# Seven-product B section in the last block, and weight-sum stores issued by GpSimd

## The chip, the cores and the metric

The kernel runs on one core of one Trainium2 chip. The metric is the device time of one execution in microseconds (us). The engines are TensorE (PE), VectorE (DVE), ScalarE (ACT), GpSimd (POOL) and SyncE (SP, which only issues DMAs here). Each engine works through its own instructions in order. They meet through semaphores.

## The reference, cut to what matters

One layer of a streaming encoder over 2048 prompt tokens and 64 sample tokens:

```
h = rmsnorm(x); proj = h @ w_in                       # 1024 -> 10240 columns
a_u,a_v,a_z, b_a,b_b,b_z, c_x,c_z, d_b,d_c,d_x,d_z, gate_logits = split(proj)
glu = b_a * sigmoid(b_b)                              # the "B" section
cb = causal_depthwise(glu, 31 taps); out_b = silu(layernorm(cb)) * silu(b_z)
...                                                   # three more branches
merged = sum_i sigmoid(gates_i) * (out_i @ w_branch_i); y = merged @ w_out
x = x + rmsnorm(y)
```

## The kernel before, in words

The tokens go in four blocks of 512 (the last one 576, with the 64 sample tokens), j = 0 to 3 in the code, called blocks one to four here. A block is 120 *units* on PE. A unit is one product of a 1024x128 weight tile with the block's activations, in three passes (high part by high part, high by low, low by high), 24 matmuls of 512 columns. A *half unit* has a 512x128 weight and 12 matmuls. The units form sections in this order: B (8 units), V (4), C (8), M (8), G0 (16, full and half alternating), D (16), G1 (16), G2 (12), Z (4), G2b (4), G3 (16), O (8). The B section gives b_a and b_b, whose product with the sigmoid is `glu`. DVE then runs the 31 taps of the depthwise convolution (`conv_step`, four DVE instructions a tap, eight in block four) wherever it has room.

From M to G3, blocks three and four use a seven-product scheme (Strassen's, in Winograd's form) in place of plain units: a *pair* of units becomes seven products of 12 matmuls with half the tokens as columns, 84 matmuls where the units need 96 of the same width. DVE adds the products in `pair_sums` (seven adds, five of which read PSUM), ACT copies the first product out of PSUM (`copy_p1`). The scheme needs sums of the activations (`t_sums`, high and low parts made by ACT and DVE in section O of the block before) and sums of the weights.

The weight sums are made once, in 60 *halves* (30 pairs by two). For each half SP loads the raw weights (`s_load`, 512 KB), POOL forms four sums (`s_sums`, four instructions), ACT casts them to the high part (`s_cast`), POOL subtracts for the low part (`s_low`), and SP stores both (`s_store`, 1 MB) to `s_parts` in DRAM, from where blocks three and four load them as `chunk`s of 512 KB through a ring of eight. Eight halves are made in block one (`HALF0`), 52 in block two, one about every two units. The order is written out by hand: lists such as `HALF_LOAD`, `HALF_STORE`, `HALF_CAST` hold, for each half, the step (a unit number) at which an engine does its part. SP's queue in block two is, step by step: the due store, the due raw load, the unit's weight load (`split_load`, up to four units ahead). A half's sums wait until the last store from the same `s_out` buffer has landed.

Of the kernel before, what the change touches and what calls it, by code (L numbers as in the profile page):

```python
# [19 lines left out]
P = 128  # L20
# [37 lines left out]
NPAIR = len(PAIRS)  # L58
NCHUNK = PAIR_CHUNK[-1]
# [7 lines left out]
NH = 2 * NPAIR  # L67
HW = WB // 2
# [6 lines left out]
SUM0 = [UNIT0["G0"] + r for r in (1, 7, 13)] + [UNIT0["G3"] - 1 + 5 * h for h in range(5)]  # L75
# [19 lines left out]
RAW_OF = [0 if h < HALF0 else (h - HALF0) % 3 for h in range(NH)]  # L95
SUM_OF = [0 if h < HALF0 else (h - HALF0) % 2 for h in range(NH)]

# [41 lines left out]

def unit_pieces(name, r):  # L140

    if name[0] == "G":
        m = GATED[name][1] + r // 2
        if r % 2:
            return [("branch", GATED[name][0] * KT + m, 0)]
        return [("main", MAIN0[name] + r // 2, c) for c in range(2)]
    return [("main", MAIN0[name] + r, c) for c in range(2)]


def chunk_stream():  # L150
# [7 lines left out]
    for j in range(SEVEN0, NBLK):  # L158
        if j > SEVEN0:
            for name, count in SECTIONS:  # L160
                if name == "M":
                    break
                for r in range(count):
# [28 lines left out]
def build(nc, x_t, x_rows, w_main, w_half, w_branch, cols, rows, bs_rows, ws_t, mask_t, pool_w, ident_in,  # L192
# [4 lines left out]
    def sb(name, shape, dt=F32, addr=None):  # L197
# [3 lines left out]
        if addr is None:  # L201
# [23 lines left out]
    s_parts = nc.dram_tensor("s_parts", (NPAIR, 2, P, 4, 2, HW), F32).ap()  # L225
# [34 lines left out]
    s_out = [sb(f"s_out{b}", [P, 4, 2, HW], F32R, addr=o) for b, o in enumerate((t2_at, raw_at))]  # L260
    s_sum = [sb(f"s_sum{b}", [P, 4, 2, HW], addr=o) for b, o in enumerate((t2_at, raw_at))]
# [3 lines left out]
             enumerate([o + TPB // 2 * DM * 4 for o in out1_at] + [at[0], at[0] + HW * 4])]  # L265
    zc = [sb(f"zc{b}", [P, WMAX]) for b in range(2)]

    a = at[0]
    ext = [sb(f"ext{b}", [P, EL]) for b in range(2)]
    sq_x = sb("sq_x", [P, WMAX], addr=a)  # L270
# [76 lines left out]
    s_loaded = [sem(f"s_loaded{b}") for b in range(3)]  # L347
    s_summed, s_hi_done = sem("s_summed"), sem("s_hi_done")
    s_lo_done, s_stored = sem("s_lo_done"), [sem(f"s_stored{b}") for b in range(2)]
# [78 lines left out]
    def banks(j, p):  # L428

        hw = half(j)  # L430
        if PAIRS[p][0] == "D" and PAIRS[p][1] % 2:
# [9 lines left out]
    def gp(j, p):  # L441
        return (j - SEVEN0) * NPAIR + p

# [11 lines left out]
    def sigs_before(j, p):  # L455
        n = sum(sigs_of(*pair) for pair in PAIRS[:p])
        return n + (j - SEVEN0) * sum(sigs_of(*pair) for pair in PAIRS)
# [53 lines left out]
    def _(sp):  # L511
# [11 lines left out]
        def s_load(h):  # L523
# [4 lines left out]
            if h == HALF0:  # L528
                sp.wait_ge(w_lo_done, UPB)
            before = [g for g in range(h) if RAW_OF[g] == RAW_OF[h]]  # L530
# [4 lines left out]
        def s_store(h):  # L535

            sp.wait_ge(s_lo_done, h + 1)
            sp.dma_start(s_parts[h // 2, h % 2, :, :, :, :], f(s_out[SUM_OF[h]])).then_inc(s_stored[SUM_OF[h]], 16)

        def sum_moves(step):  # L540

            for h in range(NH):
                if HALF_STORE[h] == step:
                    s_store(h)
            for h in range(NH):
# [75 lines left out]
        for n in range(NS):  # L621
            if n == 0:
                for b in range(2):
                    sp.wait_ge(s_stored[b], 16 * SUM_OF.count(b))
            load_chunk(n)
# [20 lines left out]
    def _(pool):  # L646
# [27 lines left out]
        def s_low(h):  # L674
# [4 lines left out]
                               ALU.subtract).then_inc(s_lo_done, 1)  # L679

# [78 lines left out]
    def _(act):  # L759
# [23 lines left out]
        def s_cast(j, u):  # L783

            for h in range(NH):
# [10 lines left out]
        def copy_p1(j, p):  # L796
# [3 lines left out]
            if p and PAIRS[p - 1][0] in "MDZ":  # L800
# [103 lines left out]
        for j in range(NBLK):  # L904
# [3 lines left out]

            u0 = ub + UNIT0["B"]
            for r in range(8):  # L910
# [16 lines left out]
                if last and r == 1:  # L927
                    for dst, src in [(lnv_g_bc, rows[0:WB]), (lnv_b_bc, rows[WB:2 * WB])]:
                        act.dma_start(dst, src.partition_broadcast(P)).then_inc(lnv_loaded, 16)
# [14 lines left out]
            for r in range(8):  # L944
# [8 lines left out]
                if r % 4 < 2:  # L953
                    done(u)
                    if j * CT + c >= 2:
                        act.wait_ge(ext_used, j * CT + c - 1)
                    pcs = pieces(j, PH)
# [1509 lines left out]
```

## Time and profile before

| what | value |
|---|---|
| median of 3 runs | 2365.47 us (2365.1 to 2366.45) |
| the profiled execution | 2366.33 us |
| its span, first to last instruction | 2364.5 us |
| mean granted TensorE clock | 0.997 |
| PE busy | 2344.5 us, 99% of the span |
| DVE, POOL, ACT busy | 69%, 30%, 19% |

The table says that PE is the bound almost throughout. The 20 us that it is not busy and the stretch at a lower clock are the only places where something other than PE's own work shows.

### The profile page before, as it was taken

The numbers are of one execution on the slowest core, as the hardware profiler recorded it, in microseconds if no ns is written. First come the engines' busy times: TensorE is split into PE (matmuls) and PEld (weight loads), VectorE is DVE, ScalarE is ACT, GpSimd is POOL, SyncE is SP. The second block draws the span as 40 slices with busy tenths as digits, with TensorE's granted clock in tenths as the row PEclk, the third lists the DMA queues.
The fourth block names the chain that finished last, engine by engine and source line by source line (L and its number), as shares of the span: only waits on it lengthen the run. The fifth ranks groups of instructions, "written<-read, shape, count | busy, mean of one in ns | idle before, by whom it ended". The sixth has DMA issues, their size and how long they took to land.

```text
span 2364.5 us, 34960 instructions
## 1 busy us (share of the span) xinstructions
PE 2344.5 (99%) x13360; PEld 2087.3 (88%) x13360; DVE 1620.4 (69%) x2407; ACT 447.8 (19%) x651; POOL 704.4 (30%) x473
## 2 busy tenths in 40 slices
PE   9999999999899999999999999999999999999998
PEld 7888888888788888888888999999898999999998
DVE  7888886855467878875457666776448766677643
ACT  5223222333112211122201100111110110011111
POOL 4537644487555866566200000000200000000000
PEclk9999999999999999999999999999999999999999
DMA  8978879898998998999676999999775688988884
GB/s 330 321 256 325 330 259 325 291 342 358 379 356 288 389 354 333 358 357 374 246 276 208 336 319 372 313 335 321 275 238 179 228 282 287 321 283 265 281 283 173
DMA packets 235460, 718.11 MB, mean 304 GB/s; under 512 B 19056, under 2 KB 20720, under 8 KB 201520
## 3 DMA queue, kind: packets, MB, share of 16 engines
q1 hardware_dynamic: 222704, 683.64, 80.9%
q10 hardware_dynamic: 12608, 32.49, 3.6%
q8 instruction: 94, 1.54, 0.2%
q14 instruction: 54, 0.44, 0.1%
HBM read 535.12 MB, written 180.94 MB: 303 GB/s over the span
## 4 chain that ended last, share of the span: by engine, by line
PE 95%; DVE 2%; issue 1%; DMA 1%; DVEq 1%; ACT 0%; POOL 0%; POOLq 0%; SPq 0%; ACTq 0%
PE acc L1951 48%; PE acc L2176 23%; PE side L2187 8%; PE side L2095 4%; PE side L2176 3%; PE acc L2335 3%; PE side L2335 3%; PE side L2123 1%; PE acc L2332 1%; PE side L2332 1%; DVE cb L1220 1%; PE side L2113 1%; PE acc L2365 0%; PE acc L2056 0%; DMA w_pair<-split_main 0%
## 5 line engine op out<-in xcount | busy, mean ns | idle before, releaser
L1951 PE MATMUL acc<-h_hi,w_pair 128*128 128x512 f32 x2592 | 816.4, 391 | 7.6 <-DMA w_pair<-split_main 7.6
L1951 PEld LDWEIGHTS acc<-h_hi,w_pair 128*128 128x128 f32 x2592 | 488.0, 188 | 109.6 <-issue 8.3
L1951 PE MATMUL acc<-h_lo,w_pair 128*128 128x512 f32 x1296 | 505.7, 390 | 0.0
L1220 DVE SCALAR_TENSOR_TENSOR cb<-glu,col,cb 128x512 f32<-128x512 f32 x600 | 457.6, 828 | 18.9 <-issue 10.9
L698 POOL TENSOR_TENSOR rstd<-msq,nhalf 128x5 f32<-128x5 f32 (+4 forms) x19 | 19.9, 1047 | 1113.3 <-DVE msq L1106 525.2
L651 POOL TENSOR_TENSOR w_pair<-w_raw,w_pair 128x1024 fp32r<-128x1024 f32 x118 | 268.9, 2290 | 230.9 <-ACT w_pair L778 214.3
L2176 PE MATMUL acc<-t_hi,chunk 128*128 128x256 f32 (+1 forms) x1520 | 300.6, 288 | 0.0
L1951 PEld LDWEIGHTS acc<-h_lo,w_pair 128*128 128x128 f32 x1296 | 244.2, 188 | 50.5
L2176 PE MATMUL acc<-h_hi,chunk 128*128 128x256 f32 (+1 forms) x1248 | 253.1, 289 | 0.4 <-DVE zc L1553 0.4
L2176 PEld LDWEIGHTS acc<-t_hi,chunk 128*128 128x128 f32 x1520 | 244.7, 189 | 0.5
L2176 PE MATMUL acc<-t_lo,chunk 128*128 128x256 f32 (+1 forms) x832 | 239.6, 288 | 0.0
L2176 PEld LDWEIGHTS acc<-h_hi,chunk 128*128 128x128 f32 x1248 | 203.6, 190 | 1.2 <-DVE zc L1553 0.6
L678 POOL TENSOR_TENSOR s_out<-s_sum,s_out 128x1024 fp32r<-128x1024 f32 x60 | 150.1, 2501 | 137.4 <-ACT s_out L789 133.7
L2176 PE MATMUL acc<-h_lo,chunk 128*128 128x256 f32 (+1 forms) x624 | 180.2, 289 | 0.0
L2187 PE MATMUL side<-out_hi,chunk 128*128 128x288 f32 (+1 forms) x768 | 173.2, 327 | 0.0
L1951 PE MATMUL acc<-out_hi,w_pair 128*128 128x512 f32 x512 | 168.6, 390 | 0.5 <-DVE merged L1516 0.5
L2176 PEld LDWEIGHTS acc<-t_lo,chunk 128*128 128x128 f32 x832 | 157.2, 189 | 0.2
L2187 PEld LDWEIGHTS side<-out_hi,chunk 128*128 128x128 f32 x768 | 124.2, 189 | 9.5
L778 ACT ACTIVATE w_pair<-w_raw 128x512 fp32r<-128x512 f32 (+1 forms) x117 | 109.8, 940 | 87.0 <-PE acc L1951 61.8
L2176 PEld LDWEIGHTS acc<-h_lo,chunk 128*128 128x128 f32 x624 | 118.4, 190 | 0.6
L1951 PEld LDWEIGHTS acc<-out_hi,w_pair 128*128 128x128 f32 x512 | 96.2, 188 | 21.2 <-DVE merged L1516 0.9
L2187 PE MATMUL side<-out_lo,chunk 128*128 128x288 f32 (+1 forms) x384 | 104.8, 327 | 0.0
(333 smaller groups left out, 3433.5 us busy)
## 6 DMA issues: line engine op xcount, KB each, us to landing
chunk<-s_parts SPq DMA_DIRECT2D x240, 512.0 KB, 6.0
chunk<-split_main SPq DMA_DIRECT2D x236, 512.0 KB, 5.8
w_pair<-split_main SPq DMA_DIRECT2D x108, 1024.0 KB, 7.1
split_main<-w_pair SPq DMA_DIRECT2D x88, 1024.0 KB, 7.4
s_parts<-s_out SPq DMA_DIRECT2D x60, 1024.0 KB, 5.5
w_raw<-in_w_main SPq DMA_DIRECT2D x88, 512.0 KB, 5.4
chunk<-split_branch SPq DMA_DIRECT2D x64, 512.0 KB, 4.4
s_raw<-in_w_half SPq DMA_DIRECT2D x60, 512.0 KB, 6.2
```

The lines of the kernel that those rows point to most:

```text
L651: pool.tensor_tensor(w_lo[s][:, 0:n], w_raw[s][:, 0:n], f(w_hi[s])[:, 0:n], ALU.subtract).then_inc(w_lo_done, 1)
L678: pool.tensor_tensor(out[:, :, 1, :], s_sum[SUM_OF[h]][:, :, 1, :], f(out)[:, :, 0, :], ALU.subtract).then_inc(s_lo_done, 1)
L778: act.activation(w_hi[s][:, 0:n], w_raw[s][:, 0:n], ACT.Copy).then_inc(w_hi_done, 1)
L1220: dve.scalar_tensor_tensor(dst, src, c1("conv_w", c * CK + t), dst, ALU.mult, ALU.add)
L1951: ins = pe.matmul(acc[:, s, b, 0:m], w_k[:, wt, wk], mv_[:, k, t0:t0 + m], start=(k == 0 and n == 0), stop=(k == nk - 1 and n == 2))
L2095: ins = pe.matmul(v_tile(t), ht[:, k, t * P:(t + 1) * P], w_k[:, wt, :], start=(r == 0 and n == 0), stop=(r == 3 and n == 5))
L2113: ins = pe.matmul(side[:, k % 2, t0:t0 + m], wt[:, c, :], part[:, c, t0:t0 + m], start=(n == 0), stop=(n == 2))
L2123: ins = pe.matmul(side[:, k % 2, t * P:t * P + n], v_n[0:n, t, c * P:(c + 1) * P], ws[0:n, c, 0:n], start=True, stop=True)
L2176: ins = pe.matmul(bank, w_k, rhs[r_part][:, k, :], start=(k == 0 and c == 0), stop=(k == CT - 1 and c == 2))
L2187: ins = pe.matmul(side[:, m % 2, t * 512:t * 512 + m_], wt[:, w_part, k * P:(k + 1) * P], rhs[:, k, t0:t0 + m_], start=(k == 0 and c == 0) ...
L2332: ins = pe.matmul(bank[:, 0:N1], wt[:, part, n * P:(n + 1) * P], act_part[:, TOK * P:WMAX], start=(k == 0 and c == 0), stop=(k == KT - 1 a ...
L2335: ins = pe.matmul(bank, act_part[:, n // 2 * P:(n // 2 + 1) * P], wt[n % 2][:, part, :], start=(k == 0 and c == 0), stop=(k == KT - 1 and ...
```

## The change

1. The B section of block four becomes four pairs in the seven-product scheme (`b_pairs` on PE, `pair_sums` and the `glu` product on DVE, `copy_p1` and the sigmoid on ACT), numbered p = -4 to -1. Its weight stream is 28 chunks instead of 16. The residual rows y of block three, which DVE finishes in this section, move to after the second, third and fourth pair, and both of their stores to its end.
2. Four more pairs need eight more halves of weight sums. They are made in block three, in sections B to C, from two new raw buffers (in the homes of `ext` and `zc`) and two new output buffers (in `out_hi[0]` and `out_lo[0]`). DVE's first C result now waits for these stores. `HALF0` is 7 instead of 8: the half that was made in section O of block one is now the first of block two.
3. SP stores no weight sums any more. POOL issues each store itself, right behind the low part.
4. ACT casts the activation sums for block four one step earlier in section O.

```diff
-SUM0 = [UNIT0["G0"] + r for r in (1, 7, 13)] + [UNIT0["G3"] - 1 + 5 * h for h in range(5)]
+SUM0 = [UNIT0["G0"] + r for r in (1, 7, 13)] + [UNIT0["G3"] - 1 + 5 * h for h in range(4)]
...
+B_CAST = [1, 3, 4, 6, 8, 9, 11, 13]
+HALF_LOAD += [SEVEN0 * UPB + r for r in (0, 1, 4, 7, 9, 10, 12, 14)]
...
-        def s_store(h):
-            sp.wait_ge(s_lo_done, h + 1)
-            sp.dma_start(s_parts[h // 2, h % 2, :, :, :, :], f(s_out[SUM_OF[h]])).then_inc(s_stored[SUM_OF[h]], 16)
...
         def sum_moves(step):
-            for h in range(NH):
-                if HALF_STORE[h] == step:
-                    s_store(h)
...
             pool.tensor_tensor(out[:, :, 1, :], s_sum[SUM_OF[h]][:, :, 1, :], f(out)[:, :, 0, :],
                                ALU.subtract).then_inc(s_lo_done, 1)
+            pool.wait_ge(s_lo_done, h + 1)
+            pool.dma_start(s_parts[h // 2, h % 2, :, :, :, :], f(out)).then_inc(s_stored[SUM_OF[h]], 16)
...
+                if j == SEVEN0:
+                    pool.wait_ge(acc_done, SEVEN0 * UPB)
+                    s_sums(NH)
                 power(TPB + 1)
+                if j == SEVEN0:
+                    for h in range(NH, NH_ALL - 1):
+                        s_low(h)
+                        if h < NH_ALL - 2:
+                            s_sums(h + 1)
                 power(TPB)
+                if j == SEVEN0:
+                    s_sums(NH_ALL - 1)
+                    s_low(NH_ALL - 1)
...
             def c_result(c):
+                if (j, c) == (SEVEN0, 0):
+                    for b in (2, 3):
+                        dve.wait_ge(s_stored[b], 16 * SUM_OF.count(b))
...
+            def b_pairs():
+                for c in range(NB):
+                    p = c - NB
+                    n, g, bank = PAIR_AT[j, p][0], gp(j, p), banks(j, p)
...
+                    product(n, h11, bank[0])
...
+                    product(n + 1, tt[2], bank[1])
...
+                    product(n + 2, tt[3], bank[2])
+                    product(n + 3, tt[1], bank[3])
...
+                    pe.wait_ge(p1_copied, g + 1)
+                    product(n + 4, h21, bank[0])
+                    pe.wait_ge(pair_summed, 6 * g + 1)
+                    product(n + 5, h22, bank[1])
+                    pe.wait_ge(pair_summed, 6 * g + 2)
+                    product(n + 6, tt[4], bank[2])
```

SP's queue at the border of blocks one and two, before: the last stores of split weights (`split_main<-w_pair`), then the raw half loads (`s_raw`), the unit weight loads (`w_pair`) and the stores of sums (`s_parts`).

```order
L521 DMA split_main<-w_pair_67 128x2048
L533 DMA s_raw_97<-in_w_half 128x1024
L552 DMA w_pair_64<-split_main 128x2048
L552 DMA w_pair_65<-split_main 128x2048
L533 DMA s_raw_98<-in_w_half 128x1024
L552 DMA w_pair_66<-split_main 128x2048
L552 DMA w_pair_67<-split_main 128x2048
L538 DMA s_parts<-s_out_100 128x2048 x2
L533 DMA s_raw_99<-in_w_half 128x1024
L552 DMA w_pair_64<-split_main 128x2048
```

The same place of the change:

```order
L547 DMA split_main<-w_pair_67 128x2048
L561 DMA s_raw_97<-in_w_half 128x1024
L572 DMA w_pair_64<-split_main 128x2048
L572 DMA w_pair_65<-split_main 128x2048
L561 DMA s_raw_98<-in_w_half 128x1024
L572 DMA w_pair_66<-split_main 128x2048
L572 DMA w_pair_67<-split_main 128x2048
L561 DMA s_raw_99<-in_w_half 128x1024
L572 DMA w_pair_64<-split_main 128x2048
```

The two stores that stood ahead of the fifth unit's weight load (`w_pair_64` the second time) are gone from SP's queue.

POOL's queue for two halves of block two, in the change: four sums, the low part, and now the store.

```order
L689 TENSOR_TENSOR s_sum_105<-s_raw_98 128x256
L691 TENSOR_TENSOR s_sum_105<-s_raw_98 128x256
L692 TENSOR_TENSOR s_sum_105<-s_raw_98,s_sum_105 128x256
L694 TENSOR_TENSOR s_sum_105<-s_raw_98,s_sum_105 128x256
L701 TENSOR_TENSOR s_out_101<-s_sum_105,s_out_101 128x4x256
L704 DMA s_parts<-s_out_101 128x2048
L689 TENSOR_TENSOR s_sum_104<-s_raw_99 128x256
L691 TENSOR_TENSOR s_sum_104<-s_raw_99 128x256
```

Before, the same five compute instructions follow each other with nothing between the low part and the next half's sums. So each half has one more POOL instruction, a DMA.

DVE's queue at the start of block four, before: the first two `glu` products (from PSUM and the sigmoid) and the first residual rows.

```order
L1278 COPY glu<-smp_g 128x4x30
L1303 TENSOR_TENSOR glu<-acc,sig_104 128x288
L1303 TENSOR_TENSOR glu<-acc,sig_104 128x224
L1303 TENSOR_TENSOR glu<-acc,sig_104 128x64
L1303 TENSOR_TENSOR glu<-acc,sig_105 128x288
L1303 TENSOR_TENSOR glu<-acc,sig_105 128x224
L1303 TENSOR_TENSOR glu<-acc,sig_105 128x64
L1190 SCALAR_TENSOR_TENSOR y_nat<-y_nat,rstd,g_half_84 128x512
```

In the change, the first pair there:

```order
L1329 COPY glu<-smp_g 128x4x30
L1338 TENSOR_TENSOR zc_114<-acc,zc_115 128x288
L1341 TENSOR_TENSOR zc_115<-acc,zc_114 128x288
L1345 TENSOR_TENSOR zc_114<-acc,zc_115 128x288
L1347 TENSOR_TENSOR zc_114<-acc,zc_114 128x288
L1348 TENSOR_TENSOR zc_115<-acc,zc_115 128x288
L1351 TENSOR_TENSOR zc_114<-acc,zc_114 128x288
L1353 TENSOR_TENSOR zc_115<-acc,zc_115 128x288
L1369 TENSOR_TENSOR glu<-zc_115,sig_108 128x512
L1369 TENSOR_TENSOR glu<-zc_115,sig_108 128x64
```

Three short instructions a pair of units became nine, and two residual rows now stand behind the last pair, ahead of the convolution.

## Rows read from the trace of the kernel before

**Rows 1.** The page's first part: busy time, share, instructions.

```profile
PE 2344.5 (99%) x13360; PEld 2087.3 (88%) x13360; DVE 1620.4 (69%) x2407; ACT 447.8 (19%) x651; POOL 704.4 (30%) x473
```

**Rows 2.** The chain that ended last: start, us, what; block starts.

```profile
589.59 21.51 PE acc L1951 x95
611.10 7.86 DMA w_pair<-split_main
...
619.10 24.69 PE acc L1951 x96
...
1176.08 43.54 PE acc L1951 x192
...
1257.70 0.68 PE side L2113 x3
...
1724.61 51.18 PE acc L1951 x384
...
1822.28 0.95 PE side L2113 x6
...
2070.84 11.14 PE acc L2176 x84
```

**Rows 3.** SP's queue in order of time, start of block two.

```profile
589.98 20.60 SPq L538 DMA_DIRECT2D s_parts<-s_out  x2
...
611.10 1.99 SPq L552 DMA_DIRECT2D w_pair<-split_main  x2
```

**Rows 4.** POOL in order of time: start, us, what, [idle before <-releaser].

```profile
603.44 0.74 POOL L666 TENSOR_TENSOR s_sum<-s_raw 128x256 f32<-128x256 f32 x1 [16.59 <-DMA s_parts<-s_out]
```

**Rows 5.** Busy us by stretch: PE, PEld, DVE, ACT, POOL, granted clock, DMA share, GB/s.

```profile
589.60:643.80 54.20, 46.64 (x193) 38.07 (x194) 22.13 (x28) 8.18 (x10) 29.99 (x26) 0.91 0.95 375
...
647.07:659.96 12.89, 12.89 (x59) 10.68 (x58) 12.73 (x12) 1.06 (x1) 7.77 (x7) 1.00 1.02 422
766.00:832.00 66.00, 65.51 (x290) 53.90 (x289) 56.19 (x45) 13.92 (x16) 53.96 (x41) 1.00 1.01 387
1402.00:1442.00 40.00, 40.00 (x339) 39.86 (x338) 28.70 (x58) 2.80 (x6) 0.00 (x0) 1.00 1.02 373
```

**Rows 6.** POOL in order of time, section G0 of block two, one half.

```profile
801.57 2.40 POOL L678 TENSOR_TENSOR s_out<-s_sum,s_out 128x1024 fp32r<-128x1024 f32 x1 [1.22 <-ACT s_out L789]
...
809.80 2.39 POOL L678 TENSOR_TENSOR s_out<-s_sum,s_out 128x1024 fp32r<-128x1024 f32 x1 [1.22 <-ACT s_out L789]
```

**Rows 7.** ACT in order of time, sections G0 and G1 of block two.

```profile
806.12 0.69 ACT L849 ACTIVATE sig<-acc,col 128x512 f32<-128x512 f32 x1 [4.62 <-PE acc L1951]
808.66 1.06 ACT L789 ACTIVATE s_out<-s_sum 128x1024 fp32r<-128x1024 f32 x1 [1.86 <-POOLq L672]
814.28 0.69 ACT L849 ACTIVATE sig<-acc,col 128x512 f32<-128x512 f32 x1 [4.55 <-PE acc L1951]
...
925.80 0.69 ACT L849 ACTIVATE sig<-acc,col 128x512 f32<-128x512 f32 x1 [3.16 <-PE acc L1951]
929.79 1.06 ACT L789 ACTIVATE s_out<-s_sum 128x1024 fp32r<-128x1024 f32 x1 [3.30 <-POOLq L672]
```

**Rows 8.** A DMA issue on ACT's queue, and POOL's shortest instruction.

```profile
1204.79 0.40 ACTq L873 DMA_DIRECT2D out_y_rows<-x_half  x1
...
1181.79 1.18 POOL L698 TENSOR_TENSOR rstd<-msq,nhalf 128x5 f32<-128x5 f32 x1 [18.89 <-DVE msq L1497]
```

**Rows 9.** DVE in order of time: block two, block three (V, C), block four.

```profile
647.07 12.89 DVE L1220 SCALAR_TENSOR_TENSOR cb<-glu,col,cb 128x512 f32<-128x512 f32 x12
...
1222.90 19.62 DVE L1220 SCALAR_TENSOR_TENSOR cb<-glu,col,cb 128x512 f32<-128x512 f32 x28
...
1252.14 0.69 DVE L1388 TENSOR_TENSOR out_lo<-pooled,out_hi 128x512 fp32r<-128x512 f32 x1
...
1777.40 2.81 DVE L1218 TENSOR_SCALAR cb<-glu,col 128x512 f32<-128x512 f32 x8
...
1819.48 0.76 DVE L1388 TENSOR_TENSOR out_lo<-pooled,out_hi 128x576 fp32r<-128x576 f32 x1
```

More of the change, by code:

```diff
@@ L58 @@
 NPAIR = len(PAIRS)
+NB = CT
+PAIR_TILE += [MAIN0["B"] + 2 * c for c in range(NB)]
 NCHUNK = PAIR_CHUNK[-1]
@@ L455, in sigs_before @@
     def sigs_before(j, p):
+        if p < 0:
+            return sum(sigs_of(*pair) for pair in PAIRS) + NB + p
         n = sum(sigs_of(*pair) for pair in PAIRS[:p])
-        return n + (j - SEVEN0) * sum(sigs_of(*pair) for pair in PAIRS)
+        return n if j == SEVEN0 else n + NB + sum(sigs_of(*pair) for pair in PAIRS)
     def unrolled(eng, j, start, end, body):
@@ L783, in s_cast @@
         def s_cast(j, u):
[L785 removed]
+            for h in range(NH_ALL):
                 if HALF_CAST[h] == u:
@@ L907, in _ @@
             q0 = j * 64
+            for c in range(NB if seven_b(j) else 0):
+                p = c - NB
+                copy_p1(j, p)
+                if c == 0:
+                    act.wait_ge(h_ready, h_count(j, KT))
+                    load_xres(j - 1)
+                act.wait_ge(pair_summed, 6 * gp(j, p) + 5)
+                act.activation(sig[0][:, 0:width(j)], zc[0][:, 0:width(j)], ACT.Sigmoid).then_inc(pair_sig, 1)
+            if seven_b(j):
+                act.wait_ge(pair_used, 2 * gp(j, 0))
+                for dst, src in [(lnv_g_bc, rows[0:WB]), (lnv_b_bc, rows[WB:2 * WB])]:
+                    act.dma_start(dst, src.partition_broadcast(P)).then_inc(lnv_loaded, 16)
+                for g in range(2):
+                    store_y(j - 1, g)
             u0 = ub + UNIT0["B"]
-            for r in range(8):
+            for r in range(0 if seven_b(j) else 8):
                 u = u0 + r
@@ L2064, in _, with product @@
             ub = j * UPB
-            for r in range(8):
+            hw = half(j)
+            h11, h21, h22 = ([h[:, c0:c0 + CT, t0:t0 + hw] for h in (h_hi, h_lo)]
+                             for c0, t0 in ((0, 0), (CT, 0), (CT, hw)))
+            tt = {n: [t_hi[j, n], t_lo[j, n]] for n in range(1, 5)} if is_seven(j) else {}
+            def product(n, rhs, bank):
+                landed(n)
+                wt = chunk[n % CHUNKS]
+                summed = STREAM[n][0] == "sum"
+                for k in range(CT):
+                    for c, (w_part, r_part) in enumerate(((0, 0), (0, 1), (1, 0))):
+                        at_half = w_part * HW + k % 2 * P
+                        w_k = wt[:, k // 2, at_half:at_half + P] if summed else wt[:, w_part, k * P:(k + 1) * P]
+                        ins = pe.matmul(bank, w_k, rhs[r_part][:, k, :],
+                                        start=(k == 0 and c == 0), stop=(k == CT - 1 and c == 2))
+                ins.then_inc(chunk_done, 1)
@@ L2066, in _ @@
+            if seven_b(j):
+                b_pairs()
+            for r in range(0 if seven_b(j) else 8):
                 u = ub + r
```

166 lines of the change are left out of this document (106 added, 60 removed).

## The prediction, made blind

> **What bounds the kernel now.** I read the page first: PE is busy for 99% of the span [rows 1], so a gain has to shorten PE's work or one of its few holes. Next the chain that ended last, block by block. The reader should compare three B sections in it [rows 2]. In block three the eight units take 43.54 us without a break. The same eight in block two take 21.51 + 7.86 + 0.14 + 24.69 = 54.2 us: between them PE waits for a DMA, the weight load of the fifth unit. The table of stretches adds that the granted clock over this section was 0.91 and PE busy 46.64 us of it [rows 5], where otherwise the clock there is at its upper level of 2.4 GHz: part of it ran at 1.2 GHz after the idle 7.6 us. So the hole costs 54.2 - 43.5 = 10.7 us, 7.6 us idle and 3.1 us of slower work.
>
> Why was that load late? SP's queue [rows 3] shows two stores of weight sums, the second stuck until 610.6 us, and the weight load issued at 611.10. POOL's own view [rows 4] closes the circle: the half whose store was awaited began its sums only at 603.44, after 16.59 us idle for the landing of the store before, which SP had issued at 589.98, long after its data were ready, because its place in SP's queue was there.
>
> **Part 1, block four's B section: -6.6 us.** Before 384 matmuls in 51.18 us [rows 2]. After, 4 pairs of 84, all with 288 columns; a pair of this kind takes 11.14 us in section D of the same block [rows 2]. 4 x 11.14 = 44.6 us. The conditions between products look met: DVE needs about 3.2 us of adds and 0.9 us for glu of a pair's 11.1, and the residual rows (1.45 us each, three at a time) fit behind. The activation sums are ready before block four starts, as the casts run in section O.
>
> What is late next is DVE. Before, it began the convolution at 1777.40, about 1.6 us after the section's end at 1775.8 [rows 2, 9]. Now two residual rows (2.9 us) stand behind the fourth pair, and the last add, sigmoid and glu end some 1.8 us after PE. The convolution starts 4.9 us behind PE, 3.3 us more than before, and DVE works without a pause from there to the first pooled result, which ended at 1820.24, while PE wanted it at 1822.28 [rows 2, 9]: 2.0 us of room. So PE waits about 3.3 - 2.0 = **+1.3 us** in section C.
>
> **Part 2, SP's queue: -10.7 us.** With both stores gone from SP, nothing ahead of the fifth unit's load waits for POOL's low parts. The raw load that stands there goes to a fresh buffer. Whether another unit then stalls: a raw load waits for the sums of three halves earlier, some 20 us old. DVE and ACT wait for PE in the sections that follow, so an earlier PE is not held by them. I take all of it.
>
> **Part 3, GpSimd issues the stores: +4.6 us.** This is the uncertain term. In section G0 of block two a half costs POOL 809.80 - 801.57 = 8.2 us from low part to low part [rows 6], and a slot (a full and a half unit) is 814.28 - 806.12 = 8.16 us [rows 7]. POOL has no slack there. Every us X that the store adds is a us of lag per slot. What the lag meets is ACT: it casts a half between two sigmoids, and PE's next full unit waits for the sigmoid. In G0 the cast ends at 809.72 and the next sigmoid starts at 814.28: 4.6 us of room, and the sigmoid itself may be 1.9 us late (a half unit of 2.72 us less its own 0.7 and a hop of 0.1). Seven halves in a row: PE loses 7X - 6.5, if that is positive. In G1 the cast ends at 930.85 and the next sigmoid is due at 925.80 + 8.16 = 933.96: 3.1 + 1.9 = 5.0 us, so 7X - 5.0. Section D between them (10.9 us a slot) lets POOL catch up. In G3 POOL's halves are shorter and start without lag: nothing for X up to 1.8.
>
> X is not in the trace: no DMA is issued by POOL. It holds a wait of POOL on its own semaphore and the issue. From below: a DMA issue on ACT takes 0.40 us [rows 8], with the hop 0.5. From above: POOL's low part of 2.4 us [rows 6], the longest thing it does in this loop. I take 1.15 us, near POOL's shortest instruction, 1.18 us [rows 8], as the issue is work of POOL itself. Then 7 x 1.15 = 8.05: 1.55 + 3.05 = 4.6 us. With 0.5 it is 0, with 2.4 it would be 10.3 + 11.8 and some in G3, about 25 us.
>
> The Trainium skill, "DMA: Bandwidth & Descriptors" (Specifications), gives about 1 us to the first byte on the gpsimd path against about 0.6 us on the sync and scalar path. By it X would be near 1.1 with the hop and the sum the same; no row here shows it.
>
> **Part 4, eight more halves in block three: +5 us.** POOL was idle there. Its sums slow DVE, whose convolution reads two operands from SBUF. Twelve convolution instructions with POOL busy 7.77 of 12.89 us took 12.89 us [rows 5, 9], 1.07 us each; 28 of them in block three with POOL idle took 19.62, 0.70 each. Those 28 fill section V. With casts at the ends of the units, POOL now has two sums, three low parts and some stores between 1222.9 and 1246.6, busy about two thirds: 22 instructions at 1.07, six at 0.70, end at 1250.8 instead of 1242.5, **8.3 us** later. The statistics behind them and the first pooled result (1252.83) follow. PE wants that at 1257.70 [rows 2, 9]: room 4.9 us, minus 8.3 and 0.6 for the last half's sums beside it: about 4 us. DVE's first C result then waits for the last store; its cast stands behind the second C unit, the store lands near 1268, some 5 us later than DVE would go on, relative to the shifted PE. Room of 5.5 us before the third pooled result covers most; I add 1 us. If the contention is half of this, 1 us; if the lag runs into section M, 9.
>
> Block one: seven stores by X on a POOL with room, nothing.
>
> **Sum.** -6.6 + 1.3 - 10.7 + 4.6 + 5 = -6.4 us. The profiled execution took 2366.33 us, so 2359.9; the median of the runs is 0.9 us below the profiled one, so **2359.1 us**. A measurement of this kernel tells about 0.2% (4.7 us) from no change.
>
> **Rivals.**
> *Cheap issue* (X below 0.75): part 3 costs nothing and POOL disturbs less in block three, 3 us. -6.6 + 1.3 - 10.7 + 3 = -13, 2352.5. For it: ACT's 0.40 us. Chance 0.2.
> *Dear issue, slower or no gain*: POOL's store costs 2 us. G0 7.5, G1 9, G3 about 3, block three 6: +25.5 - 16 = +9.5, 2375. The sign turns where 14X - 11.5 + 5 = 16, X = 1.6. For it: POOL's store is followed by sums that read SBUF beside a DVE 85% busy (56.19 of 66 us) [rows 5], and its instructions already stretch there. Chance 0.22.
> The Trainium skill, "SBUF — State Buffer" (the box on "DVE blocks DMA"), says that GpSimd cannot write descriptors while DVE runs a copy or cast in a two-port mode. That would be one way to this rival; casts of DVE are rare in G0 and common in the O and V sections.
> *The DMA engines bound the new B section*: 28 chunks of 512 KB and the 2.5 MB of residual rows in 44.6 us are 17.2 MB, 385 GB/s. In the stretch 1402 to 1442 the engines gave 373 GB/s at a share of 1.02 [rows 5], full. At that rate 46.1 us, 1.5 us more; bunched at the front, where eight buffers give some 6 us of room, up to 5 and then a spell at 1.2 GHz, 3. Against it: the load is even and the ring full at the start. 2360.6 to 2367. Chance 0.12.
> *The hole in block two stays*: the raw load takes the store's place in front of the weight load and waits for sums. Against it: its buffer is new. 2370. Chance 0.05.
> The forecast: 0.41.
>
> **The numbers.** Range 2350 to 2373: it reaches down past the cheap issue and up to X near 1.9. Forecast alone, X from 0.9 to 1.4 and block three 2 to 8: 2355 to 2364. Faster by over 0.2% (below 2360.7): all of the cheap case, 0.26 of the forecast's 0.41, 0.04 of the DMA case and some of the rest, together 0.52. Within: 0.23. Slower: most of the dear case, the rest of the others, 0.25.
>
> **What would show it.** Block two's B section at 43.5 us with clock 1.00 (part 2). Block four's at 44.6 us (part 1) and a short PE wait in its section C. On POOL, the gap from low part to the next sum in G0: that is X. In G0 and G1, PE waits for ACT's sigmoid behind a late cast; none means X below 0.75. In block three the 28 convolution instructions near 28 us instead of 19.6, and PE's pause ahead of the first L2113 job of section C. I am wrong if X is outside 0.75 to 1.6, or if POOL's work does not slow DVE.

## The result: 2546.4 us against 2365.5, slower by 7.6%

The changed kernel took 2546.41 us (2544.72 to 2549.15 in four runs), the kernel before 2365.53 us beside it: a ratio of 1.0761, interval 1.0749 to 1.0774. The profiled execution took 2549.15 us, its span 2547.4 us. The forecast of 2359.1 and its range to 2373 were wrong by far more than any rival allowed.

The page's first part and its slices, of the kernel after, answer to [rows 1]. Each digit is the busy share of a slice in tenths; PEclk is the clock granted to TensorE.

```profile
PE 2397.7 (94%) x13312; PEld 2113.9 (83%) x13312; DVE 1618.9 (64%) x2431; ACT 455.1 (18%) x663; POOL 745.9 (29%) x581
...
PE   9999999999798898898897799999999999999999
...
PEclk9999999999899899899898899999999999999999
...
q0 software_dynamic: 9792, 71.31, 6.8%
```

PE has 48 matmuls less, but is idle for 150 us of its span where it was idle for 20, and busy 53 us longer, at a lower clock. The slices with 7 and 8 run from the eleventh to the twenty-third: block two and the start of block three, the stretch in which GpSimd makes weight sums and now issues their stores (the queue q0). POOL itself is hardly busier than before: 745.9 us against 704.4. Something stands still there.

POOL in order of time in section G0 of block two, kernel after (start, us, instruction, [idle before <-releaser]), answers to [rows 6]:

```profile
828.82 2.36 POOL L701 TENSOR_TENSOR s_out<-s_sum,s_out 128x1024 fp32r<-128x1024 f32 x1 [1.21 <-ACT s_out L825]
831.48 0.57 POOL L704 DMA_DIRECT2D s_parts<-s_out  x1 [0.29 <-POOL s_out L701]
832.07 0.74 POOL L689 TENSOR_TENSOR s_sum<-s_raw 128x256 f32<-128x256 f32 x1
835.82 0.74 POOL L691 TENSOR_TENSOR s_sum<-s_raw 128x256 f32<-128x256 f32 x1 [3.02 <-issue]
...
839.35 2.41 POOL L701 TENSOR_TENSOR s_out<-s_sum,s_out 128x1024 fp32r<-128x1024 f32 x1 [1.22 <-ACT s_out L825]
842.06 0.57 POOL L704 DMA_DIRECT2D s_parts<-s_out  x1 [0.29 <-POOL s_out L701]
842.65 0.74 POOL L689 TENSOR_TENSOR s_sum<-s_raw 128x256 f32<-128x256 f32 x1
849.34 0.72 POOL L691 TENSOR_TENSOR s_sum<-s_raw 128x256 f32<-128x256 f32 x1 [5.94 <-issue]
...
852.82 2.36 POOL L701 TENSOR_TENSOR s_out<-s_sum,s_out 128x1024 fp32r<-128x1024 f32 x1 [1.21 <-ACT s_out L825]
```

The issue is cheap: from the low part's end at 831.18 to the first sum behind the store are 0.89 us. The first sum (L689) runs at once. The second (L691) comes 3.0 and 5.9 us late, and between the two stands nothing but `pool.drain()`. A half takes 10.5 and 13.5 us from low part to low part, against 8.2 before, in a slot of 8.16 [rows 6, 7]. The group of all these second sums in the kernel after, with the idle time ahead of them behind the second bar, shows the size:

```profile
L691 POOL TENSOR_TENSOR s_sum<-s_raw 128x256 f32<-128x256 f32 x68 | 52.2, 767 | 303.5 <-issue 303.4
L704 POOL DMA_DIRECT2D s_parts<-s_out x68 | 39.4, 579 | 20.0 <-POOL s_out L701 20.0
```

That is 303 us over 67 stores, 4.5 us each, under "issue", a wait for which the profile names no releaser. The landings name it. For the two stores above, issue to landing (us) is:

```profile
DMA to landing us min/median/max: 4.2/4.2/4.2
...
DMA to landing us min/median/max: 7.1/7.1/7.1
```

831.48 + 4.2 = 835.7, and the sum starts at 835.82; 842.06 + 7.1 = 849.2, and the sum starts at 849.34. In 58 of 67 stores the second sum begins 0.17 us behind the landing; in the other nine GpSimd did other work first or waited for an input. The profile also holds the drain itself, an instruction of GpSimd's sequencer that the order of time above leaves out. The two behind these stores (line, xcount, ns min/median/max, first and last start):

```profile
L690 POOLq DRAIN  x2: 4188/5656/7125, 831.5 to 842.1; - x2
```

They last 4.2 and 7.1 us. In all 58 cases this drain's record ends 0.08 us behind the landing.

PE's longest waits in the kernel after (us in total, times, longest) show how this reaches it:

```profile
PE acc L2028 <- ACT sig L885: 57.6, 15, 6.2
PE acc L2028 <- ACTq L989: 34.5, 4, 15.0
```

ACT casts each half between two sigmoids, its cast waits for the sums, and PE's next unit waits for the sigmoid behind it (L885) or, in section V, for the drain with which ACT hands back its PSUM bank (L989). The rest of the loss is the clock. In G0 the granted clock was 1.00 and PE busy 65.5 of 66 us before [rows 5]; after, the stretch of 800 to 880 us has a clock of 0.84 and PE busy 59.2 of 80 us (span; PE, PEld, DVE, ACT, POOL busy; clock, DMA share, GB/s):

```profile
800.00:880.00 80.00, 59.19 (x223) 46.89 (x222) 29.33 (x33) 11.43 (x14) 39.36 (x40) 0.84 0.73 272
```

### The profile page after: what moved, and what is told of

It is laid out like the page before. It is cut to its first block, busy times and chain, and to the rows that moved or that the text cites. A ratio compares the mean times of both kernels' runs of the same rounds, so it can differ in the third digit from the quotient of the medians.

```text
span 2547.4 us, 35039 instructions
## 1 busy us (share of the span) xinstructions
PE 2397.7 (94%) x13312; PEld 2113.9 (83%) x13312; DVE 1618.9 (64%) x2431; ACT 455.1 (18%) x663; POOL 745.9 (29%) x581
## 4 chain that ended last, share of the span: by engine, by line
PE 63%; issue 14%; POOL 9%; POOLq 6%; DVE 4%; ACT 3%; DMA 1%; DVEq 1%; ACTq 0%; SPq 0%
PE acc L2156 23%; PE acc L2028 21%; PE side L2297 7%; POOL s_out L701 6%; PE side L2156 3%; PE acc L2445 2%; PE side L2445 2%; ACT s_out L825 2%; POOLq L695 2%; POOLq L690 2%; POOLq L693 2%; POOL s_sum L691 2%; DVE cb L1271 1%; POOL s_parts L704 1%; PE side L2223 1%
## 5 line engine op out<-in xcount | busy, mean ns | idle before, releaser
L2028 PE MATMUL acc<-h_hi,w_pair 128*128 128x512 f32 x2592 | 852.0, 405 | 117.8 <-ACT sig L885 57.6
L2028 PEld LDWEIGHTS acc<-h_hi,w_pair 128*128 128x128 f32 x2592 | 509.4, 197 | 239.1 <-ACT sig L885 41.5
L1271 DVE SCALAR_TENSOR_TENSOR cb<-glu,col,cb 128x512 f32<-128x512 f32 x600 | 439.5, 798 | 18.9 <-issue 10.9
L2156 PE MATMUL acc<-t_hi,chunk 128*128 128x256 f32 (+1 forms) x1648 | 327.8, 288 | 2.2 <-DMA chunk<-s_parts 2.2
L2156 PE MATMUL acc<-h_hi,chunk 128*128 128x288 f32 (+1 forms) x1344 | 273.5, 289 | 0.4 <-DVE zc L1338 0.4
L2156 PEld LDWEIGHTS acc<-t_hi,chunk 128*128 128x128 f32 x1648 | 265.5, 189 | 3.1 <-DVE zc L1338 1.5
L2156 PE MATMUL acc<-t_lo,chunk 128*128 128x288 f32 (+1 forms) x896 | 258.2, 288 | 0.0
L2156 PE MATMUL acc<-h_lo,chunk 128*128 128x288 f32 (+1 forms) x672 | 194.0, 289 | 0.0
L825 ACT ACTIVATE s_out<-s_sum 128x1024 fp32r<-128x1024 f32 x68 | 72.0, 1058 | 597.7 <-POOLq L695 593.8
L691 POOL TENSOR_TENSOR s_sum<-s_raw 128x256 f32<-128x256 f32 x68 | 52.2, 767 | 303.5 <-issue 303.4
L1625 DVE TENSOR_TENSOR tmp<-acc,sig 128x512 f32<-128x512 f32 x48 | 33.2, 692 | 166.3 <-ACT sig L885 83.0
```

What stands on the lines that cost most here:

```text
L691: pool.tensor_tensor(s1, a22, a21, ALU.add)
L825: act.activation(out[:, :, 0, :], s_sum[b][:, :, 1, :], ACT.Copy).then_inc(s_hi_done, 1)
L1271: dve.scalar_tensor_tensor(dst, src, c1("conv_w", c * CK + t), dst, ALU.mult, ALU.add)
L2028: ins = pe.matmul(acc[:, s, b, 0:m], w_k[:, wt, wk], mv_[:, k, t0:t0 + m], start=(k == 0 and n == 0), stop=(k == nk - 1 and n == 2))
L2156: ins = pe.matmul(bank, w_k, rhs[r_part][:, k, :], start=(k == 0 and c == 0), stop=(k == CT - 1 and c == 2))
```

## The experiments

Eleven kernels were run. All times are medians; the kernel before took 2365.8 to 2366.4 us beside them.

**Stores back on SyncE.** The changed kernel, in which GpSimd's issue is replaced by SyncE's (`s_store` is defined again as in the kernel before):

```diff
+            for h in range(NH_ALL):
+                if HALF_STORE[h] == step:
+                    s_store(h)
-            pool.wait_ge(s_lo_done, h + 1)
-            pool.dma_start(s_parts[h // 2, h % 2, :, :, :, :], f(out)).then_inc(s_stored[SUM_OF[h]], 16)
```

> The changed kernel with the stores of the weight sums issued by SyncE again, at the steps that its list still holds; the seven products of block four's section B, the seven early halves and the eight more halves stay. Theory (A): the whole loss comes from a GpSimd instruction behind the GpSimd-issued store that stands until the store has landed (in the trace of the changed kernel a store is issued at 831.48 and lands 4.2 us later, and the second sum behind it begins at 835.82; the next is issued at 842.06, lands 7.1 us later, and the second sum begins at 849.34). Then this kernel has none of it: 2366.3 - 6.6 + 1.3 + 5.0 by the recorded steps one and four, the hole in block two stays, so 2366, 2355 to 2373. Rival (B): the seven products and the eight more halves cost much of it: over 2400.

Measured: 2368.09 us, ratio 1.0007 (0.9997 to 1.0016). The whole loss of 178 us hangs on who issues the stores.

**GpSimd's stores alone.** The kernel before, `s_store` and its loop taken from SyncE and this put at the end of `s_low`:

```diff
+            pool.wait_ge(s_lo_done, h + 1)
+            pool.dma_start(s_parts[h // 2, h % 2, :, :, :, :], f(out)).then_inc(s_stored[SUM_OF[h]], 16)
```

> The kernel before, with one edit: GpSimd issues each store of a half behind its low part, SyncE none. Theory (A): 59 or 60 stores stall GpSimd some 4.5 us each (303.5 us over 67 in the changed kernel), and block two and three lose as in the changed kernel: 2520, 2490 to 2550. Rival (B), that block four's section B is the cause: 2352 to 2380.

Measured: 2498.96 us, ratio 1.0552 (1.0523 to 1.0582), 132.6 us slower. GpSimd stands for 244.4 us in 59 gaps ahead of the second sum. Rival (B) is out.

**No drains.** The changed kernel, with semaphore waits in the drains' place:

```diff
-            pool.tensor_tensor(s3, a21, a11, ALU.subtract)
-            pool.drain()
+            pool.tensor_tensor(s3, a21, a11, ALU.subtract).then_inc(s_step, 1)
+            pool.wait_ge(s_step, 2 * h + 1)
             pool.tensor_tensor(s1, a22, a21, ALU.add)
-            pool.tensor_tensor(s2, a22, s3, ALU.add)
-            pool.drain()
+            pool.tensor_tensor(s2, a22, s3, ALU.add).then_inc(s_step, 1)
+            pool.wait_ge(s_step, 2 * h + 2)
-            pool.tensor_tensor(s4, a12, s2, ALU.subtract)
-            pool.drain().then_inc(s_summed, 1)
+            pool.tensor_tensor(s4, a12, s2, ALU.subtract).then_inc(s_summed, 1)
```

> The changed kernel, GpSimd still issues the stores, but the three drains between the sums are gone: the sum that needs the one before it waits for a semaphore that this one raises. Theory (A), that it is a drain behind the issue that stands until the transfer has landed: the time behind the issue is 1 us or less, and the kernel comes out where the prediction's sum put it, 2359, 2350 to 2373. Rival (C): GpSimd is itself taken up by making the transfer's descriptors, and one instruction only slipped past it: the sums still stand 3 to 10 us behind each store, 2500 to 2550. Rival (D), that GpSimd-issued stores slow SyncE's loads in the DMA engines: time stays over 2400 though GpSimd's gaps are gone.

Measured: 2381.85 us, ratio 1.0068 (1.0051 to 1.0084): 164.6 of the 178 us are gone though GpSimd still issues 68 stores. POOL in order of time, this kernel:

```profile
827.89 0.57 POOL L704 DMA_DIRECT2D s_parts<-s_out  x1 [0.30 <-POOL s_out L701]
828.48 0.92 POOL L690 TENSOR_TENSOR s_sum<-s_raw 128x256 f32<-128x256 f32 x1
829.48 0.73 POOL L692 TENSOR_TENSOR s_sum<-s_raw 128x256 f32<-128x256 f32 x1
```

The second sum follows 0.08 us behind the first. So GpSimd was not busy with the transfer, and rival (C) is out; at 2382 so is (D), which asked for over 2400. The time is still 9 us above the top of my range, and 14 us above the first run. The run with six stores on SyncE takes up about half of that. A further 1.9 us stands at the very end, in the one drain that is left there, with which every engine closes the program:

```profile
L2492 POOLq DRAIN  x1: 6234/6234/6234, 2374.7 to 2374.7; - x1
```

The last store had landed 1100 us earlier, so this is no wait for a landing. With no GpSimd transfer since the drain before it the closing drain took 0.66 us, with one 0.75 (the changed kernel), and with 60, 62 and 68, in the three kernels here that issue on GpSimd and have no other drain behind it, 5.58, 5.75 and 6.23: 0.08 us for each transfer.

**A small transfer.** The first run's kernel, with this at the end of `s_low`:

```diff
+            pool.dma_start(probe[h, :, :], nhalf[:, :]).then_inc(probed, 16)
```

> The kernel of the first run (stores by SyncE), and GpSimd issues behind each low part a transfer of 4 KB (128 rows of 32 bytes) to a DRAM tensor that nobody reads; this adds work and leaves none out. Theory (A): the second sum stands until that small transfer has landed, so the gap ahead of it follows the landing of this transfer, some 2 to 3 us from issue, less 1.3 for the issue and the first sum: 1 to 2 us instead of 3 to 7, and the kernel loses 0 to 60 us to the first run. Rival (E): any GpSimd-issued transfer costs the drain a fixed time: the gap's mean is again near 4.5 us and the kernel is at 2520 to 2550. Rival (C'), that making 1 MB of descriptors takes the time: gap under 0.5 us.

Measured: 2460.81 us, ratio 1.0403 (1.0386 to 1.0421). The transfer is of 128 rows of 32 bytes, from a constant. The time lies 33 us above my range: the rule held, my estimate of the landing did not. POOL in order of time, and the landings of all 68:

```profile
830.57 0.56 POOL L713 DMA_DIRECT2D probe<-nhalf  x1
831.15 0.74 POOL L699 TENSOR_TENSOR s_sum<-s_raw 128x256 f32<-128x256 f32 x1
835.75 0.74 POOL L701 TENSOR_TENSOR s_sum<-s_raw 128x256 f32<-128x256 f32 x1 [3.87 <-issue]
```

```profile
DMA to landing us min/median/max: 4.7/5.0/6.8
```

These 4 KB take no less time to land than the 1 MB store does in a quiet moment (4.2 us), not the 2 to 3 us that I had expected. In 58 of the 67 the second sum again begins 0.17 us behind the landing. The gaps of 3.4 us on average, 227 us in all, cost 92.7 us against the first run. So most of the stall does not depend on the size of the transfer, and one that nobody reads causes it too. Rivals (E) and (C') are out.

**Only the last drain.** As the run without drains, but the third drain stays:

```diff
             pool.tensor_tensor(s4, a12, s2, ALU.subtract)
             pool.drain().then_inc(s_summed, 1)
```

> The changed kernel with only the last of the three drains kept: the first two are semaphore waits as in the third run. Theory (A), a drain stands until the store issued ahead of it has landed: now all four sums run first, behind the issue, and the last drain ends at the landing. A half's period is then landing plus about 4.2 us instead of landing plus about 6.3, so some 2.1 us less for each of the 53 halves of block two and a few of block three: 2546 less 110 to 130, near 2430, 2400 to 2460, and the stretch from the start of the last sum to the cast behind it ends 0.2 us or so behind the landing. Rival (C): the second drain, or the count of drains, carries the stall: either 2380 (no stall) or 2546 (all of it).

Measured: 2437.27 us, ratio 1.0297 (1.0281 to 1.0312), 109 us less than with three drains. All four sums now run behind the issue, and the wait has moved to the kept drain, behind which ACT's cast and then the low part stand. POOL in order of time, this kernel:

```profile
826.04 0.57 POOL L705 DMA_DIRECT2D s_parts<-s_out  x1 [0.29 <-POOL s_out L702]
...
829.76 1.07 POOL L695 TENSOR_TENSOR s_sum<-s_raw,s_sum 128x256 f32<-128x256 f32 x1
836.52 2.37 POOL L702 TENSOR_TENSOR s_out<-s_sum,s_out 128x1024 fp32r<-128x1024 f32 x1 [5.70 <-ACT s_out L826]
```

This store lands 9.2 us after its issue, at 835.3, and the cast starts at 835.4. Rival (C) is out: neither none of the stall nor all of it is left.

**ScalarE's drain.** The first run's kernel with a drain in `store_y`:

```diff
             act.dma_start(rows_view(y_rows, j * TPB + a // 2, 2), x_half[g][:, :, :]).then_inc(y_stored, 16)
+            act.drain()
```

> The kernel of the first run with a drain on ScalarE behind each of its own stores of the output (1 MB, x_half to y_rows) in the first three blocks. If a drain stands until the engine's own transfers have landed on any engine, ScalarE's next instruction, ready in this trace 0.1 to 1.4 us behind the issue, begins some 6 to 10 us later, and the kernel is slower than 2368 by 0 to 30 us. If only GpSimd's (software) queue does it, nothing moves: 2368.

Measured: 2367.30 us, ratio 1.0007, the same as the first run. The six stores of this kernel that have the drain behind them land 8.7 to 11.9 us after their issue, and each of the six drains takes 0.16 to 0.17 us. ACT in order of time, one of them; the next instruction starts 0.70 us behind the issue:

```profile
1203.13 0.40 ACTq L915 DMA_DIRECT2D out_y_rows<-x_half  x1
1203.83 0.60 ACT L891 ACTIVATE sig<-acc 128x512 f32<-128x512 f32 x1 [9.36 <-PE acc L2035]
```

**Seven early halves, nothing else.** The kernel before with the change's line in SUM0:

```diff
-SUM0 = [UNIT0["G0"] + r for r in (1, 7, 13)] + [UNIT0["G3"] - 1 + 5 * h for h in range(5)]
+SUM0 = [UNIT0["G0"] + r for r in (1, 7, 13)] + [UNIT0["G3"] - 1 + 5 * h for h in range(4)]
```

> The kernel before with one edit: seven halves in block one instead of eight, so that 53 are made in block two; its B section stays plain and SyncE issues the stores. In the run with SyncE's stores the changed kernel's hole of block two (7.6 us idle and the low clock behind it) was gone although SyncE still carries the stores, so the recorded step two has its cause wrong. Theory (A): the hole goes with the eighth early half (its steps of load and store in block one and two), so this kernel takes 2366.4 - 10.1 = 2356, 2354 to 2358. Rival (B): it went with something else of the change (the eight halves' loads or the store's steps), and the hole stays: 2366.

Measured: 2355.98 us, ratio 0.9958 (0.9944 to 0.9971). It is 9.8 us faster than the kernel before, clear of the noise, and it keeps SyncE's stores. SP's queue in order of time, this kernel, answers to [rows 3]:

```profile
600.49 0.32 SPq L538 DMA_DIRECT2D s_parts<-s_out  x1
600.85 0.43 SPq L533 DMA_DIRECT2D s_raw<-in_w_half  x1
601.33 2.56 SPq L552 DMA_DIRECT2D w_pair<-split_main  x2
```

One store instead of two in a row: the weight loads behind it go out at 601.33, where before the second store held them until 611.10 [rows 3].

**Section B's sums left out.** The first run's kernel, with work left out, so that its outputs are not those of the layer: GpSimd does no sums and low parts for seven of the eight halves of section B (both stand under `if not left_out(h):`), and ScalarE fills both parts from the raw rows:

```diff
+                    if left_out(h):
+                        act.activation(out[:, :, 1, :], s_raw[RAW_OF[h]][:, :, :], ACT.Copy)
+                        act.activation(out[:, :, 0, :], s_raw[RAW_OF[h]][:, :, :], ACT.Copy).then_inc(s_hi_done, 1)
+                        continue
```

> The kernel of the first run (stores by SyncE), with the sums and the low parts of the first seven of the eight halves for block four's section B left out on GpSimd; ScalarE writes both parts from the raw rows, so that loads, stores and waits stay. The output of block four is another one for that. Theory (A): GpSimd's instructions slow the convolution on VectorE beside them (28 multiply-adds took 29.24 us there, 19.62 before), and this made the 10.8 us wait of TensorE ahead of block three's pooling product and the low clock behind it: now near 20 us, no wait, 2368.1 - 13.3 = 2355, 2353 to 2358. Rival (B): the late landing of the doubled row g_half (21.5 us, the DMA engines at over 0.9) made it: the convolution is fast again but starts late as before, and 2358 to 2364 is left. Rival (C): the DMA traffic slows VectorE itself: 29 us and 2368 stay.

Measured: 2354.73 us, 13.4 below the first run. The 28 multiply-adds of block three's convolution in DVE's order of time, in the first run's kernel and then in this one (start, us for all 28):

```profile
1217.64 29.24 DVE L1277 SCALAR_TENSOR_TENSOR cb<-glu,col,cb 128x512 f32<-128x512 f32 x28
```

```profile
1213.57 19.62 DVE L1289 SCALAR_TENSOR_TENSOR cb<-glu,col,cb 128x512 f32<-128x512 f32 x28
```

PE's wait of 10.8 us ahead of the pooling product is gone with them. Rival (C) is out. The stretches of the convolution, slow and fast (span; busy time of PE, PEld, DVE, ACT, POOL; clock, DMA share, GB/s):

```profile
1217.64:1246.88 29.24, 29.24 (x131) 24.21 (x130) 28.79 (x29) 3.32 (x4) 16.57 (x11) 1.00 1.00 393
```

```profile
1213.57:1233.19 19.62, 19.62 (x88) 16.27 (x87) 19.17 (x29) 5.13 (x6) 0.00 (x0) 1.00 1.01 423
```

The DMA engines are as full beside the fast one. Rival (B) is not separated fully: the row g_half landed after 8.1 to 9.7 us here, 16.3 to 21.5 in the first run, so the convolution also began on time again. In the first run the first pooled result comes 15.7 us later than here: 4.1 by the convolution's start, 9.6 by its own slowing, 2.0 by a cast (below).

**Six stores on SyncE.** The kernel without drains; the first six stores of block two by SyncE, the other 62 by GpSimd, with semaphores of their own for the six:

```diff
+    def of_sp(h):
+        return HALF0 <= h < HALF0 + 6
...
+            if not of_sp(h):
+                pool.wait_ge(s_lo_done, h + 1)
+                pool.dma_start(s_parts[h // 2, h % 2, :, :, :, :], f(out)).then_inc(s_stored[SUM_OF[h]], 16)
```

> The kernel of the third run (no drains, stores by GpSimd, 2381.9), but the first six stores of block two are issued by SyncE at their listed steps, the other 62 by GpSimd. Theory (A): in block two's section B SyncE's queue, no longer held by a store's wait, lets loads and stores pile onto the DMA engines, and the row g_half for VectorE lands 25.6 us after its issue, so TensorE waits 5.3 us and runs at the low clock behind it, 7.6 us in all; with the waits back in SyncE's queue these 7.6 us go: 2374, 2372 to 2377. Rival (B): those 7.6 us come from GpSimd's own work or its later stores: 2380 to 2383.

Measured: 2375.99 us, ratio 1.0042 (1.0027 to 1.0058). The row g_half, issued by ACT near 596 us; issue to landing in the first run, the third run, and this one:

```profile
DMA to landing us min/median/max: 7.4/7.6/7.8
```

```profile
DMA to landing us min/median/max: 20.4/23.0/25.6
```

```profile
DMA to landing us min/median/max: 7.5/7.6/7.6
```

In the third run PE had waited 5.3 us for the glu that stood behind it in DVE's order, and 7.6 us were lost in all; here none is. SP's queue shows what differs: in the third run the next weight loads go out at once, here they stand behind a store that waits for its low part. SP in order of time, third run, then this one:

```profile
594.92 5.76 SPq L573 DMA_DIRECT2D w_pair<-split_main  x2
```

```profile
600.92 0.32 SPq L579 DMA_DIRECT2D s_parts<-s_out  x1
601.28 0.43 SPq L574 DMA_DIRECT2D s_raw<-in_w_half  x1
601.76 2.51 SPq L593 DMA_DIRECT2D w_pair<-split_main  x2
```

From 595 to 600 us, while ACT's rows were to come in, the DMA share was 1.01 in the third run and 0.88 here. So a wait in SyncE's queue had kept loads off the DMA engines. The store itself is issued at nearly the same time in both (600.75 and 600.92), but by another engine's queue; that this queue matters as well is not excluded.

**Drains without GpSimd stores, and the reverse.** Two kernels, both on top of the seven early halves: the three drains replaced as above with SyncE's stores kept, and the same with the stores in `s_low`. The edits are those of the runs above.

> The kernel before with seven early halves (2356.0) and GpSimd's three drains between the sums replaced by semaphores; stores by SyncE. Theory (A): the drains cost nothing where no GpSimd-issued transfer stands ahead (their gaps are 0.13 us each), so 2356, 2355 to 2357. Rival: the sums' 0.1 to 0.3 us a half open a cover somewhere: 2353 to 2355.

Measured: 2355.80 us, ratio 0.9956 (0.9943 to 0.9970), the same as with drains.

> The same with the stores issued by GpSimd behind each low part, no drain anywhere on GpSimd's way: the change's third part alone, mended. Theory (A): what is left of its cost is the issue (0.57 + 0.30 us a half on GpSimd) and block two's section B, where the unpaced queue lets the row g_half land late (7.6 us of the 12.5 in the third run), then some 3 to 5 us more: 2356 + 7.6 + 2 to 5 = 2366, 2361 to 2371. Rival: with the issue off SyncE's queue and no drain this beats the plain one: under 2355.

Measured: 2367.03 us (2363.19 to 2372.5, a wider spread than the others'), ratio 1.0007 (0.9998 to 1.0016). Even without a drain the stores on GpSimd are worth nothing: 11 us worse than SyncE's. The row g_half lands after 16.4 and 23.0 us here. The trace is of the fastest of the eleven executions and shows 7.5 us of the 11: 6.2 up to the last matmul, the rest behind it, where the closing drain takes 5.58 us.

## Why the prediction was wrong, step by step

To place the times, I count TensorE's instructions and compare when the same one starts in two profiled executions. Us by which each is later than the kernel before (from the end of block four's B on the 48 matmuls fewer are allowed for; "end" is the last matmul):

```
starts                      first run   changed   no drains, 6 SyncE
end of block two's B        -10.5       -4.1      -10.8
start of block three        -10.1       +139.8    -7.6
behind its pooling product  +4.2        +179.6    +9.4
start of block four         +4.2        +183.3    +9.4
end of block four's B       +0.4        +179.5    +5.6
in its section C            +2.5        +183.2    +7.4
end                         +2.2        +182.8    +7.2
```

**Part 3, the issue on GpSimd, is the step that failed.** Its X was defined as what the store adds between low part and next sum, taken as 1.15 us, and it measured 0.89. The sum by this formula would be 7 x 0.89 - 5.0 = 1.2 us. (With X = 1.1, which the part calls the same sum, it is 3.9 instead of 4.6.) X even lay inside the 0.75 to 1.6 us outside of which I would have called myself wrong. What the step missed is that the sums themselves hold drains, and that a drain behind a GpSimd-issued transfer stands until it has landed: 4.5 us more per half. The part listed a wait and the issue as all that the store adds, and no word on the drains, though they stand in the code between L689 and L694. With 0.89 + 4.5 = 5.4 us a half the limits to sections G0 and G1 fall too. From low part to low part a half of block two then takes 12.9 us on average (10.5 to 24.4), against 9.9 in the first run, and section D's slots of 10.9 us no longer let POOL catch up. Block two's halves cost PE 150 us against the first run up to block three, and the eight of block three 29 us. Removing the drains, keeping one, and adding a transfer of 4 KB to SyncE's stores moved the time as that rule says (2382, 2437, 2461), and drains beside SyncE's stores cost nothing (2356.0 with, 2355.8 without).

*Dear issue* named the right side, with another mechanism and a seventh of the price (25.5 us for 180.7). The Trainium skill, "SBUF — State Buffer" (the box on "DVE blocks DMA"), would put the delay on descriptors that GpSimd cannot write while DVE holds the port. The runs do not show that here: without drains the sums went on at once, and in the changed kernel GpSimd's store landed in 4.2 us where no other load was under way. No run sets such a DVE instruction against a GpSimd issue, so the rule itself is not tried.

**Part 2, -10.7, had the right size, and credited one of two items that each remove the hole.** The first run and the kernel with seven early halves gain 10.5 and 10.4 us there with the stores still in SyncE's queue. The hole came from two stores in a row, the first with its landing awaited by POOL, the second stuck behind that half's low part; with one early half fewer there is one store. The step's own reason holds as well: in the kernel before with GpSimd's stores, which keeps eight early halves, SP issues the fifth unit's load at 596.68 instead of 611.10, and PE waits there for ACT instead. So the gain was to be had without moving a single store; in the first run it is the other item that gives it. In the changed kernel itself GpSimd's stall took 6.4 us of it back in the same section.

**Part 4, +5, was the right mechanism, too small.** I had the 28 convolution instructions at "near 28 us"; they took 29.24. Without the sums beside them they take 19.62. But PE lost 13.3 us there in the first run, not 5. Two things had been left out. The convolution started 4.8 us late: DVE stood idle for 6.6 us until the row g_half had landed, 21.5 us after its issue, and the eight residual rows behind it, with instructions of 0.7 us each, were slowed beside GpSimd's sums and low parts just as the convolution was. And a cast in the pooled result took 2.41 instead of 0.43 us beside a low part. DVE in order of time, the first run's kernel, one instruction of a residual row and that cast:

```profile
1206.29 2.92 DVE L1247 SCALAR_TENSOR_TENSOR y_nat<-y_nat,rstd,g_half 128x512 f32<-128x512 f32 x1
...
1256.02 2.41 DVE L1492 CAST out_hi<-pooled 128x512 fp32r<-128x512 f32 x1
```

PE then waited 10.8 us, and the rest of the 13.3 is work at the lower clock behind it. GpSimd's low parts beside the two, in POOL's view of the same kernel:

```profile
1206.27 2.40 POOL L709 TENSOR_TENSOR s_out<-s_sum,s_out 128x1024 fp32r<-128x1024 f32 x1 [1.57 <-ACT s_out L831]
...
1255.41 2.73 POOL L709 TENSOR_TENSOR s_out<-s_sum,s_out 128x1024 fp32r<-128x1024 f32 x1 [1.22 <-ACT s_out L831]
```

The Trainium skill, "SBUF — State Buffer" (section "SBUF: two separate sides"), describes the port shared by GpSimd and VectorE as an exclusive lock held for a whole instruction; the trace agrees: the cast begins 0.6 us into a low part of 2.73 us and ends 0.3 us behind it; the row's instruction begins 0.02 us behind the start of one and ends 0.5 us behind its end.

**Part 1, -6.6 + 1.3.** The price of a pair was right: in the first run three of the four pairs took 11.1 us each. The second took 14.0, so the section gained 3.8 us and not 6.6. In it PE waits 1.4 us for a chunk of sums and 0.7 us for DVE, and some matmuls run slower behind these waits. Section C's wait was 1.9 us, forecast 1.3 (2.1 lost with the clock). PE's waits there, the first run's kernel:

```profile
PE side L2247 <- DVE out_lo L1494: 1.9, 1, 1.9
PE acc L2162 <- DMA chunk<-s_parts: 1.4, 1, 1.4
PE acc L2162 <- DVE zc L1344: 0.7, 1, 0.7
```

That is mostly the *DMA* rival, at 2.8 of the 1.5 to 8 us that it allowed: the load of that chunk took 13.4 us. So the seven products are worth about 2 us net in block four (from +4.2 to +2.2) and cost 14 in block three.

The other steps as measured by the first run make -10.5 + 0.4 + 14.3 - 2.0 = +2.2 without part 3, and part 3 is +180.7.

What stays open is part of the 7.9 us by which the run with six SyncE stores is slower than the first (medians; 6.4 in the profiled executions). Of those 6.4 us, 1.4 stand behind the last matmul, where the closing drain takes 5.75 us. The other 5.0 arise in block two behind section G0 and in block three (+2.9 and +2.7; 0.6 is won back elsewhere). Whether these are GpSimd's issue time or its stores' traffic, no run tells.

## What to carry to other kernels

Before a transfer is moved to GpSimd's queue, look for drains in what GpSimd does next: here the first one behind each store made it a blocking call until its landing, with 1.8 to 10.8 us of idle time, and 4 KB instead of 1 MB shortened it only from 4.5 to 3.4 us on average; a semaphore on the one operand that matters did not block. A wait in an in-order queue of loads may be what keeps the DMA engines free for somebody else's rows, so taking it away can move the stall instead of ending it. And when a change has several parts, the gain can hang on a number that nobody named: here one early half fewer gives the 10 us by itself.

## What the hardware showed that I had not expected

A drain on GpSimd waits for the landing of GpSimd's own DMA: its record ends 0.08 us behind the landing in 58 of 67 cases, and the next instruction starts at 0.17. A drain on ScalarE behind ScalarE's own DMA does not (0.16 us, landing 8.7 us or later). GpSimd's drain also takes 0.08 us for each of its DMAs since the drain before, landed long ago or not: 6.23 us with 68 behind it, 0.66 with none. A GpSimd-issued transfer of 4 KB in 128 rows of 32 bytes landed in 5.0 us (median), 1 MB in 4.2 at the least and 6.8 in the median.
